# Attention masks of a hybrid layer: from matmuls on TensorE to additions on VectorE

## What is computed

```python
s_s = einsum('bkgqd,bkqnsd->bkgqns', qc, ks) - slopes6 * d_s
p_s = masked_softmax(s_s, d_s >= 0)                    # selected
m_w = (d_w >= 0) & (d_w < WINDOW) & (w_pos >= 0)       # window
p_c = masked_softmax(s_c, d_c >= 0)                    # compressed
out = gc[..., 0:1] * o_c + gc[..., 1:2] * o_s + gc[..., 2:3] * o_w
```

## Time and profile before

| | us |
|---|---|
| three runs, median (lowest to highest) | 1520.31 (1517.73 to 1522.61) |
| the profiled execution, its own time | 1520.41 |
| its span, from the first to the last instruction | 1518.7 |
| first sweep, its first matmul to its last maximum | 289.7 to 348.2 |
| first key phase | 353.8 to 464.7 |
| second sweep, second key phase | 482.9 to 540.5, 546.5 to 657.3 |

### The profile page before, as it was taken

The page is one execution under the profiler, slowest core; times in us unless marked ns, Lnnn a source line. Parts: engine busy times, 40 slices in busy tenths (PEclk is TensorE's granted clock), DMA queues, the critical chain, the costliest instruction groups (busy, mean ns, idle before and its releaser), DMA issues.

```text
span 1518.7 us, 17439 instructions
## 1 busy us (share of the span) xinstructions
PE 1449.0 (95%) x6656; PEld 1149.8 (76%) x6670; DVE 719.8 (47%) x882; ACT 446.1 (29%) x625; POOL 65.9 (4%) x56
## 2 busy tenths in 40 slices
PE   7999999999897998989989999999999999999995
PEld 6788888876565765668868888888888888888874
DVE  6433512496564955653353434344343434434356
ACT  5211101405776047842132111212112121111211
POOL 0010000001110001110020000000000000000000
PEclk9999999799997999999989999999999999999997
DMA  5111120000000030012102110211111111110102
GB/s 207 55 62 42 56 97 0 9 1 3 1 1 6 1 114 0 1 56 70 42 14 69 42 56 28 65 45 46 50 41 55 55 42 44 53 49 34 55 0 110
DMA packets 18686, 67.62 MB, mean 45 GB/s; under 512 B 2088, under 2 KB 2856, under 8 KB 18472
## 3 DMA queue, kind: packets, MB, share of 16 engines
q1 hardware_dynamic: 18396, 66.03, 12.9%
q0 software_dynamic: 240, 0.93, 0.4%
HBM read 63.01 MB, written 4.19 MB: 44 GB/s over the span
## 4 chain that ended last, share of the span: by engine, by line
PE 88%; DVE 5%; issue 3%; POOL 2%; ACT 1%; DMA 1%; DVEq 0%; SPq 0%; ACTq 0%; POOLq 0%
PE PS L319 18%; PE PS L320 18%; PE PS L323 18%; PE PS L1195 5%; PE PS L1199 5%; PE PS L1196 5%; PE PS L1021 3%; PE PS L1022 2%; PE PS L1117 2%; PE PS L1118 2%; PE PS L1119 1%; PE PS L1098 1%; PE PS L1099 1%; DVE nmax L774 1%; PE PS L1003 1%
## 5 line engine op out<-in xcount | busy, mean ns | idle before, releaser
L319 PE MATMUL PS<-R,wh 128*128 128x512 f32 x1200 | 470.6, 392 | 17.0 <-DVE wl L311 11.3
L320 PE MATMUL PS<-R,wh 128*128 128x512 f32 x1200 | 469.0, 391 | 0.0
L323 PE MATMUL PS<-R,wl 128*128 128x512 f32 x1200 | 371.1, 391 | 0.0
L319 PEld LDWEIGHTS PS<-R,wh 128*128 128x128 f32 x1200 | 226.5, 189 | 66.5 <-DVE wl L311 11.7
L320 PEld LDWEIGHTS PS<-R,wh 128*128 128x128 f32 x1200 | 226.6, 189 | 47.5 <-issue 0.5
L323 PEld LDWEIGHTS PS<-R,wl 128*128 128x128 f32 x1200 | 226.4, 189 | 47.4
L304 ACT ACTIVATE wh<-raw 128x1024 fp32r<-128x1024 f32 x97 | 102.0, 1051 | 260.3 <-PE PS L1199 174.0
L909 DVE TENSOR_TENSOR F<-PS,F 128x1024 f32<-128x1024 f32 x88 | 107.6, 1223 | 92.0 <-PE PS L1199 92.0
L1195 PE MATMUL PS<-R,wh 128*128 128x512 f32 x352 | 137.0, 389 | 1.1 <-DVE wl L311 1.1
L1196 PE MATMUL PS<-R,wh 128*128 128x512 f32 x352 | 136.9, 389 | 0.0
L826 DVE TENSOR_TENSOR wl<-raw,wh 128x512 fp32r<-128x512 f32 x148 | 102.8, 697 | 60.9 <-ACT raw L570 59.3
(11 more groups left out here) (141 smaller groups left out, 1372.0 us busy)
## 6 DMA issues: line engine op xcount, KB each, us to landing
raw<-in_w_units SPq DMA_DIRECT2D x97, 512.0 KB, 3.4
F<-in_xT SPq DMA_DIRECT2D x16, 512.0 KB, 8.4
outT<-F SPq DMA_DIRECT2D x8, 512.0 KB, 3.1
F<-in_w_cmp SPq DMA_DIRECT2D x1, 2048.0 KB, 7.7
masks<-in_masks POOLq DMA_DIRECT2D x1, 448.0 KB, 4.9
R<-in_alibi_q POOLq DMA_DIRECT2D x2, 160.0 KB, 4.5
R<-R SPq DMA_DIRECT2D x4, 48.0 KB
R<-in_alibi_k POOLq DMA_DIRECT2D x1, 136.0 KB, 3.5
```

Of the source, the lines that this page charges most:

```text
L319: nc.tensor.matmul(out, w_h, hi(kt)[:, cols], start=first, stop=False)
L320: nc.tensor.matmul(out, w_h, lo(kt)[:, cols], start=False, stop=False)
L323: last = nc.tensor.matmul(out, w_l, hi(kt)[:, cols], start=False, stop=end)
```

## The change

All masks leave TensorE. The mask matmuls of both phases and the constants for them go. In the sweep `tensor_reduce` becomes `tensor_tensor_reduce`: it adds a row of a bf16 mask in SBUF to the scores in PSUM, writes the result back in place, negated, and gives the minimum to `nmax`. The three forms of mask are laid out so that one slice fits each tile. In the key phase DVE adds the mask of a masked step in place to its 128x512 score tile before ACT may read it (`mask_tile`), for step s + 2 ahead of the subtraction of step s; ACT waits for it on a new semaphore, `masked`. The compressed branch's masks come as a further 512 KB float32 constant `CM`, by a DMA on POOL's queue ahead of `alibi_q`. Besides this, `unit_scores` streams only the columns that are used, and the loops over the head groups are written out as Python loops on all engines, so that semaphore targets and offsets become constants.

```diff
-NEG = -1e30
+NEG = -2.0 ** 100
...
+            pool.dma_start(CM, cmp_masks_d).then_inc(masks_in, 16)
-            with <every engine>.Fori(0, KV) as g:
+            for g in range(KV):
...
                 def max_of(b, br, unit, col, count):
-                    return nc.vector.tensor_reduce(nmax[:, br, i, h:h + 1],
-                                                   pair(2 * (b % 2) + unit)[:, col:col + count], AX.X, ALU.max,
-                                                   negate=True)
+                    row = pair(2 * (b % 2) + unit)[:, col:col + count]
+                    bias = {0: M_SEL + T - count, 1: M_WIN if i >= WT else M_SEL + T - count,
+                            2: M_CMP + 8 * (TT - 1 - i)}[br]
+                    return nc.vector.tensor_tensor_reduce(row, row, masks[:, bias:bias + count], -1.0, -2 * NEG, ALU.add,
+                                                          ALU.min, nmax[:, br, i, h:h + 1])
+                if g == 0:
+                    dve.wait_ge(masks_in, 32)
...
+                def mask_tile(s):
+                    mask = mask_of(s)
+                    if mask is None:
+                        return
+                    dve.wait_ge(st_ready, NS * g + s + 1)
+                    scores = PS[:, s % 4, :].rearrange("p (h q) -> p h q", h=GROUP)
+                    nc.vector.tensor_tensor(scores, scores, mask.rearrange("p (o q) -> p o q", o=1)
+                                            .broadcast_to([P, GROUP, P]), ALU.add).then_inc(masked, 1)
+                mask_tile(0)
+                mask_tile(1)
                 for s in range(NS + 6):
+                    if s + 2 < NS:
+                        mask_tile(s + 2)
                     if s < NS:
                         dve.wait_ge(e_ready, NS * g + s + 1)
...
                         act.wait_ge(st_ready, NS * g + s + 1)
+                        if mask_of(s) is not None:
+                            act.wait_ge(masked, masked_upto(g, s))
...
-                        scores(bank + c // BANK, 0, h, i, key + c, min(BANK, KEYS - key - c),
-                               any(c <= col < c + BANK for col in masked_cols))
+                        last = scores(bank + c // BANK, 0, h, i, key + c, min(BANK, width - c))
...
-                    if mask is not None:
-                        last = nc.tensor.matmul(out, masks[:, mask:mask + P], masks[:, M_ID:M_ID + GROUP * P],
-                                                start=False, stop=True)
```

More of the change, by code:

```diff
@@ L189, in f32, with mask_of, masked_upto @@
             return ap.bitcast(F32)
+        def mask_of(s):
+            i, br, j = STEPS[s]
+            if br == 2:
+                return f32(CM[:, i * P:(i + 1) * P])
+            if j == i:
+                return masks[:, M_TILES:M_TILES + P]
+            return masks[:, M_TILES + P:M_TILES + 2 * P] if br == 1 and j == i - WT else None
+        def masked_upto(g, s):
+            tiles = [n for n in range(NS) if mask_of(n) is not None]
+            return len(tiles) * g + sum(n <= s for n in tiles)
         consts_in, late_in, w1_in, ak_in = sem("consts_in"), sem("late_in"), sem("w1_in"), sem("ak_in")
         masks_in, params_in = sem("masks_in"), sem("params_in")
+        masked = sem("masked")
         g_hi, g_lo, r_ready, conv_ready, tapr_ready = (sem("g_hi"), sem("g_lo"), sem("r_ready"), sem("conv_ready"),
@@ L439, in _ @@
             pool.dma_start(KB[DH:DH + AR + MR, :], alibi_k).then_inc(ak_in, 16)
-            with pool.Fori(0, KV) as g:
+            pool.dma_start(CM, cmp_masks_d).then_inc(masks_in, 16)
+            for g in range(KV):
                 pool.dma_start(QB[DH:DH + AR, :, :, :].rearrange("r i h q -> r (i h q)"),
@@ L517, in _ @@
             act.wait_ge(unit_lo, N_IN + 1)
-            with act.Fori(0, KV) as g:
+            for g in range(KV):
                 def kv_rows(what, half):
@@ L741, in _ @@
             nc.vector.tensor_copy(posb[:, :], PS[:, 7, BANK // 2:BANK // 2 + 2]).then_inc(posb_ready, 1)
-            with dve.Fori(0, KV) as g:
-                steps.enter(g, KV, 2 * TT)
+            for g in range(KV):
                 for half in range(2):
@@ L997, in _ @@
             pe.wait_ge(clear_ready, 5)
-            with pe.Fori(0, KV) as g:
+            for g in range(KV):
                 def compressed_hidden(kv, src, pairs=range(CMP_BLOCK // 2)):
@@ L1015, in _, with scores, unit_scores @@
                 pe.wait_ge(k_lo, 4 * g + 4)
[L1018 removed]
+                def scores(bank, col, h, i, key, count):
                     out = PS[:, bank, col:col + count]
                     nc.tensor.matmul(out, QA[:, i, h, :], KA[:, key:key + count], start=True, stop=False)
[L1022 to L1025 removed]
+                    return nc.tensor.matmul(out, QB[0:DH + AR, i, h, :], KB[0:DH + AR, key:key + count], start=False,
+                                            stop=True)
+                def unit_scores(bank, h, i, key, width):
                     for c in range(0, width, BANK):
[L1029 to L1035 removed]
+                        last = scores(bank + c // BANK, 0, h, i, key + c, min(BANK, width - c))
+                    return last
                 for b in range(NR):
@@ L1312 @@
     first = lambda a: np.asarray(a)[0].reshape(16, P, P).transpose(1, 0, 2).reshape(P, 2, 1024)
-    consts, masks, aq, ak = _shape_constants()
+    consts, masks, cmp_masks, aq, ak = _shape_constants()
     arrays = {
@@ L1318 @@
         "w_cmp2": A(np.stack([np.asarray(w_ck2)[0], np.asarray(w_cv2)[0]], axis=1)),
-        "params": A(params), "consts": consts, "masks": masks, "alibi_q": A(aq), "alibi_k": ak,
+        "params": A(params), "consts": consts, "masks": masks, "cmp_masks": cmp_masks, "alibi_q": A(aq), "alibi_k": ak,
     }
```

55 lines of the change are left out of this document (21 added, 34 removed).

## The result

Four runs of the changed kernel have a median of **1543.94 us** (1537.22 to 1552.31), four of the kernel before on the same chip 1519.02 us. The ratio to it is 1.017, 95% interval 1.0137 to 1.0204: slower by 1.7%, 25 us. I had forecast slower and 1536 us, with a range of 1512 to 1556. The profiled execution took 1544.8 us (span 1542.5), 24 us more than that of before.

The account below looks back on a forecast made before the run. It took TensorE and DVE as close to balance in the sweeps and TensorE as leading in the key phases. 1520.4 + 0 (sweep) + 19 (key phase) + 3 (clock) - 6 (loop) = 1536 us, range 1512 to 1556.

Parts of the forecast that it names:

- X: Sweep: extra DVE time per masked reduction for its accumulator output, taken as 0.09 us, ends 0 and 0.19.
- 1, the sweep: Both sweeps: DVE becomes the bound, 58.5 us a sweep against 58.5 now; term 0, ends -17 and +19.
- DVE's floor: Sweep: DVE's least time with plain reductions, overlaps taken off and six query instructions added: 48.8 us.
- The 0.7 and 0.4 for its start and its gaps: Sweep: DVE starts 0.7 us after PE's first matmul, and 0.4 us is left for its gaps.
- PE stops being the bound: Sweep: without 112 mask matmuls and with fewer columns, TensorE needs about 41 us, so DVE has to be costed.
- 2, the key phase: Both key phases: masks on DVE ahead of the subtraction stall TensorE, +9.4 us a pass; term +19.
- isolated stalls, copies, turns: Key phase, a pass: stalls at masked steps 7.8 us, masks meeting DVE's output copies 4, masks between invert and scale 4.5.
- the walk through the queues: Key phase: four engine queues followed through all 74 steps, 106.1 us for the old order and 115.5 for the new.
- 3, the clock: Key phases: more holes make another fall of TensorE's clock likely in about one of two passes; +3 us, ends 0 and +15.
- a rival at 0.07: Clock stays at 1.2 GHz in the sweep, TensorE's 66 us bound it, key phases lose again: about 1551 us; chance 0.07.
- 4, the loop: Between the passes: writing the loop out removes a 5.8 us restart; term -6, ends -3 and -7.
- 5, the rest: Outside the phases: the 512 KB load of CM is covered and ScalarE's added waits are already counted; no term.

Follow-up runs that it names:

- e_unroll: The kernel before with its loop over the two key-value heads written out on every engine, masks still on TensorE: 1511.26 us, ratio 0.9958.
- e_key_nomask: The kernel after without any mask in the key phase, mask data and the queries' ALiBi rows zero: 1519.32 us, ratio 1.0025 to before.
- e_wide_sub: e_wide with the mask of step s+2 behind the subtraction of step s, ScalarE's accumulation left five steps behind the turn: 1523.68 us, ratio 1.0047.
- e_wide_acc7: e_wide with ScalarE's accumulation of a turned query tile seven steps behind the turn, not five: 1508.75 us, ratio 0.9924 to before.
- e_wide: The kernel after, but TensorE streams 512 key columns where the tile needs fewer, as before did: 1526.11 us, ratio 1.0086 to before.
- e_unroll_acc7: e_unroll with ScalarE's accumulation seven steps behind the turn, not five: 1497.19 us, ratio 0.9859 to before.
- e_unroll_narrow: e_unroll with only the used key columns streamed in the sweep, masks on TensorE, plain reductions: 1506.26 us, ratio 0.9904 to before.

## Why the prediction was right, and where it was not

The direction and the range held; the median lies 8 us above the number. That it is only 8 is luck in part: with the X that was measured my sum would have given 1528. The steps:

- **1, the sweep: the cost on DVE was right in kind and too high, the bound was wrong.** The Trainium skill ("VectorE: DVE Perf Modes", section "Two Vector instructions with no wait between them") says that an op which writes out its accumulator is two instructions. The trace agrees: 96 reads of 140 ns. The masked reduction cost 0.05 us more than the plain one, not 0.09. DVE's floor was right: 48.8 us, and in the plain form DVE is busy for 48.38. The 0.7 and 0.4 for its start and its gaps were too little: it idles for 2.9 us there, so that the plain sweep took 51.3 us, not 49.9. With X = 0.05 my sum gives 54.7 us, and 56.1 was measured where the clock held. But in after it was not DVE that bounded. "PE stops being the bound" was worked out from TensorE's work at full clock, 41 us; at half clock it is the bound again. That is the step that failed.
- **2, the key phase: right.** Forecast +9.4 us a pass, measured +9.3 and +8.5; the stall of an isolated masked step 0.39 against 0.43 us. Against e_unroll, which has no restart of the loop either, it is +9.3 in both passes. The naive saving of 6.5 us of TensorE came to 1 to 2 (e_key_nomask). What my text gives as separate items (isolated stalls, copies, turns) isn't additive, as the two edits of e_wide_sub and e_wide_acc7 show: the walk through the queues, which takes a maximum at each step, was close where the granted clocks were the same: +9.4 against +9.3 for the change, 1.6 against 1 to 2 for leaving out TensorE's masks, 7.0 against 7.1 and 6.9 for the late accumulation in the order of before, 9.3 against 10.4 and 9.7 on top of the change. It was short where the place of the mask moved: 4.1 against 6.4 and 6.7, 0.7 against 2.7 and 2.6, 1.2 against 2.2 and 2.4; how much of that is the clock's stays open.
- **3, the clock: the mechanism was a rival at 0.07, its term 3 was mis-sized.** After less e_wide is 12.8 us in the sweeps and 2.1 in the seam behind the first, against my +3. I had put the fall of the clock into the key phases, where it stayed at 0.95 and 0.94. My argument against the rival was that the phases of before keep 0.94 to 0.96 in spite of their holes. Holes were the wrong measure: after's low clock lasted through 30 us without one, and the wide sweeps kept 0.94 and 0.96 with 2.8 us of them. The Trainium skill ("TensorE: Matmul & The Clock Gate", section "A second HAM failure mode: psum-queue depth-cycling") describes a kernel whose TensorE idles briefly and often between groups of matmuls, so that its clock goes back and forth between the two levels. The sweeps of after agree in part: no wait of TensorE above 0.9 us, and 0.50, 1.00 and 0.50 in turn. But e_wide's waits are of the same size and its clock held at 0.94 and 0.96, so brief idling alone doesn't explain it here. Which property of the narrow stream does, these runs leave open.
- **4, the loop: right**, 6.2 us in e_unroll against 5.8. Late next is `alibi_q`, not DVE; I had looked for that load only in the first pass.
- **5, the rest: right as far as it goes.** The 3.1 us before the first sweep stand against a term of 0. The other kernels with `CM` start their first sweep at 289.6 to 290.0 us, as before does at 289.7, while e_unroll_acc7, without `CM` or a mask on DVE, starts at 292.8. So this is a difference between executions, not the load of `CM`.

The sum with the measured sizes, in the measure of the table: sweeps at full clock -2.5 and -1.5 (55.2 against 57.7 and 56.7), the clock in them +8.2 and +5.8, key phases +8.4 and +8.0, the middle -6.2 and -0.9, the seams, from the start of the last maximum, +2.6, the start +3.1, behind the second pass -1.2: +23.8, the difference of the two spans. Two errors partly met: X too high by 0.04 x 192 = 8 us, the clock too low by 11 in the sweeps alone.

## What to carry to other kernels

Before work moves from a busy engine to an idle one, ask whether the busy one is bound by its work or by a wait: here two lines that put one ScalarE instruction two steps later were worth 7 to 10 us a pass, where taking all masks off TensorE, with the wait still there, was worth 1 to 2, and only with them is TensorE's work the bound. In an in-order queue an added instruction can cost by its place alone, even on an engine with idle time to spare: the same 28 masks cost 6.5 us a pass less behind the subtraction than ahead of it. And if TensorE is made shorter than the engine that it feeds, look at its granted clock: cutting the columns of one branch only (53.9 and 54.2 us a sweep) was better in these traces than cutting all (55.3 and 56.0).

And before one trace is set against another, ask how much the same instructions differ between two executions: here up to 2.7 us in a key phase and 8.8 in a narrow sweep.

## What the runs showed of the hardware

- Streaming fewer columns can take longer. The same sweep took 56.4 and 55.2 us with 512-column matmuls and 63.4 and 61.0 with those cut to the used width.
- TensorE's granted clock stayed at 0.50 from 293 to 322 us of after while its records leave no gap. Behind the stall of 2.78 us in before it came back within some 2 us of work that looked just as busy. What tells the two cases apart these runs don't show.
- What the low clock costs isn't fixed: two passes through the same instructions took 52.7 and 61.5 us (e_unroll_narrow), and 56.2 and 61.0 (e_key_nomask). The same key phase took 106.2 us at a clock of 0.95 (e_unroll) and 103.5 at 0.98 (e_unroll_narrow).
- The read of DVE's accumulator has a record of 140 ns and begins with the next instruction's record. With the second input and the write to PSUM it costs 50 ns an instruction.
- A DVE addition that writes to PSUM in place took 0.70 us for 512 columns, 0.60 from its start to the next, no dearer than the subtraction that writes to SBUF.
